# Weighing the oldest unit ahead of the newest unit's scores in a software-pipelined attention kernel

## The reference

```
def first_block(x, mem, ...):
    mem_n = layer_norm(mem, mem_ln_g, mem_ln_b)
    for i in range(DEPTH):                       # kinds A, B, C, A
        q, k, v, ..., qm = split_cols(x @ w_in, ...)      # with rope on q and k
        mix = dsa_attention | dilated_attention | moba_attention   (q, k, v)
        mk, mv = jnp.split(mem_n @ w_mem_kv[i], 2, axis=-1)
        mo = memory_attention(qm, mk, mv)
        mixed = jnp.concatenate([mix, mo], -1) @ w_out[i]
        x = layer_norm(ALPHA * x + mixed, ln1_g[i], ln1_b[i])
        x = layer_norm(ALPHA * x + swiglu(x, w_gate_up[i], w_down[i]), ln2_g[i], ln2_b[i])

def memory_attention(q, mk, mv):
    logits = jnp.einsum('bshd,bnhd->bhsn', q, mk) * (HEAD_DIM ** -0.5)
    p = jax.nn.softmax(logits, axis=-1)
    return jnp.einsum('bhsn,bnhd->bshd', p, mv)
```

## Time and profile before

| what | value |
|---|---|
| median of 3 runs | 1559.26 us (1557.5 to 1559.66) |
| span of the profiled execution, first to last instruction | 1558.9 us |
| PE busy | 1537.2 us (99%) |
| DVE busy | 1084.7 us (70%) |
| ACT busy | 757.7 us (49%) |
| chain that ended last | PE 85%, DVE 8%, ACT 3% |
| granted TensorE clock, mean | 0.998 |

### The profile page before, as it was taken

One profiled execution on the slowest core, in us unless ns is written; L12 is line 12 of the kernel. 1 busy time (PEld: TensorE's weight loads), 2 busy tenths in 40 slices (PEclk: granted clock), 3 DMA queues, 4 the chain that ended last, 5 costly groups with the idle time before them and its releaser, 6 DMA issues.

```text
span 1558.9 us, 19900 instructions
## 1 busy us (share of the span) xinstructions
PE 1537.2 (99%) x8187; PEld 1274.7 (82%) x8187; DVE 1084.7 (70%) x1422; ACT 757.7 (49%) x963; POOL 52.7 (3%) x89
## 2 busy tenths in 40 slices
PE   9999999999999999999999999999999999999997
PEld 7887788888878888888788888877888888978986
DVE  6876967656677776675966756888767677567764
ACT  5646544443444434346644343566444434474463
POOL 1100000000000000000000000000100000000010
PEclk9999999999999999999999999999999999999999
DMA  8752567645425766452476664533766546433530
GB/s 317 246 205 79 204 230 256 268 163 189 163 82 197 274 246 255 147 202 96 176 243 243 243 221 152 202 109 136 266 256 233 225 164 223 162 110 147 217 122 27
DMA packets 45898, 299.87 MB, mean 192 GB/s; under 512 B 5540, under 2 KB 5796, under 8 KB 12528
## 3 DMA queue, kind: packets, MB, share of 16 engines
q1 hardware_dynamic: 39600, 278.74, 48.9%
q0 software_dynamic: 5776, 19.01, 3.7%
q10 hardware_dynamic: 432, 0.85, 0.1%
HBM read 296.20 MB, written 2.65 MB: 192 GB/s over the span
## 4 chain that ended last, share of the span: by engine, by line
PE 85%; DVE 8%; ACT 3%; issue 2%; DMA 1%; SPq 0%; POOL 0%; POOLq 0%; DVEq 0%; ACTq 0%
PE psum L1305 53%; PE psum L1264 15%; PE psum L1299 7%; PE psum L1164 3%; DVE w_low L1779 2%; PE psum L1234 1%; PE psum L1428 1%; PE psum L1321 1%; PE psum L1382 1%; PE psum L1416 1%; PE psum L1302 1%; ACT w_high L1533 1%; DMA kv_outside<-arena 1%; DVE xt_low L1813 0%; DVE x_rows L1877 0%
## 5 line engine op out<-in xcount | busy, mean ns | idle before, releaser
L1533 ACT ACTIVATE w_high<-w_raw 128x2048 fp32r<-128x2048 f32 (+1 forms) x240 | 456.5, 1903 | 236.2 <-DMA w_raw<-in_weights 148.9
L1779 DVE TENSOR_TENSOR w_low<-w_raw,w_high 128x2048 fp32r<-128x2048 f32 (+2 forms) x240 | 530.0, 2214 | 34.1 <-ACT w_high L1533 33.3
L1305 PE MATMUL psum<-w_high,xt_high 128*128 128x512 f32 (+1 forms) x1376 | 379.3, 396 | 1.0 <-DVE x_rows L1877 0.8
L1305 PE MATMUL psum<-w_high,xt_low 128*128 128x512 f32 (+1 forms) x1376 | 368.8, 388 | 0.3 <-DVE xt_low L1813 0.3
L1305 PE MATMUL psum<-w_low,xt_high 128*128 128x512 f32 (+1 forms) x1376 | 368.1, 388 | 0.0
L1305 PEld LDWEIGHTS psum<-w_high,xt_low 128*128 128x128 f32 x1376 | 257.9, 188 | 54.9 <-DVE xt_low L1813 0.7
L1305 PEld LDWEIGHTS psum<-w_low,xt_high 128*128 128x128 f32 x1376 | 257.4, 188 | 53.9 <-DVE w_low L1765 0.4
L1305 PEld LDWEIGHTS psum<-w_high,xt_high 128*128 128x128 f32 x1376 | 250.4, 189 | 51.9 <-DVE x_rows L1877 2.4
L2109 DVE TENSOR_TENSOR arena<-arena,psum 128x256 f32<-128x256 f32 x88 | 37.0, 420 | 203.9 <-ACT arena L1665 203.5
L1665 ACT ACTIVATE arena<-psum 128x256 f32<-128x256 f32 x88 | 33.7, 383 | 217.6 <-PE psum L1305 217.6
L1264 PE MATMUL psum<-w_high,ht_high 128*128 128x512 f32 x352 | 99.9, 401 | 0.0
(11 more groups left out here) (250 smaller groups left out, 1486.2 us busy)
## 6 DMA issues: line engine op xcount, KB each, us to landing
w_raw<-in_weights SPq DMA_DIRECT2D x260, 1024.0 KB, 4.8
norm_params<-in_ln_g POOLq DMA_DIRECT2D x8, 512.0 KB, 4.1
norm_params<-in_ln_b POOLq DMA_DIRECT2D x8, 512.0 KB, 5.7
w_raw<-in_weights SPq DMA_DIRECT2D x4, 656.0 KB, 6.0
kv_outside<-arena POOLq DMA_DIRECT2D x3, 512.0 KB, 5.6
mem_kv<-kv_outside POOLq DMA_DIRECT2D x3, 512.0 KB, 3.6
norm_params<-mods_outside POOLq DMA_DIRECT2D x3, 512.0 KB, 6.7
x_rows<-in_x SPq DMA_DIRECT2D x4, 256.0 KB, 5.3
```

Source lines behind the costliest of these rows:

```text
L1305: m = e.matmul(psum[:, bank, 0:w], rows[:, kk, rb * P:rb * P + P], right[:, at:at + w], start=first, stop=last)
L1533: e.activation(K.w_hi[:, g % RING, 0:w], K.w_raw[:, r, 0:w], ACT.Copy).then_inc(K.high.hit(t), 1)
L1779: m = e.tensor_tensor(K.w_lo[:, s, 0:n], K.w_raw[:, r, 0:n], K.w_hi[:, s, 0:n].bitcast(F32), ALU.subtract)
```

## The change

One line in `pipelined` gets another order. A unit's generator stops after each of its stages, and each entry of the tuple lets one of the three units go one stage on.

```
-            for unit in (middle, new, oldest, new, middle, new):
+            for unit in (middle, oldest, new, new, middle, new):
                 if unit:
                     next(unit, None)
```

## The result

The change made the kernel slower: 1568.7 us (median of 4 runs, 1565.69 to 1571.72) against 1559.39 us before, ratio 1.0065 with a 95% interval of 1.0052 to 1.0078. The forecast was 1560.4 us with a range that ended at 1563.4. Five later runs of the same order gave 1570.46 us, ratio 1.0077 (1.0065 to 1.0090).

The account below looks back on a forecast made before the run. PE held 85% of the chain, with ACT and DVE holding parts of the attention layers. Two A layers +0.74, C +0.87, B -0.43 and the last two layers nothing made +1.2 us: 1560.4 us, range 1555.8 to 1563.4.

Parts of the forecast that it names:

- needs the transposed probabilities that DVE copies: Kind C, fifth round: the weighing right behind the product waits for L2080's copies; row maxima come +0.87 us later.
- 0.09 in the third: Kind A layers, third round: PE gains 0.09 us because transposes following masks need no switch of tile shape.
- gains of 0.27 + 0.09 and 0.11: Kind A layers, PE's chain: first round gains 0.27 + 0.09 us, second 0.11.
- the 0.93 of the fourth round: Fourth A round: row maxima 1.02 - 0.09 = 0.93 us later; less earlier gains of 0.56, the layer ends +0.37.
- In B -0.43: Kind B: 1.66 us wait goes, but the last unit's later softmax delays its transposes; the product starts 0.43 us earlier.
- 0.87 + 2.19: The 0.87: kind C's fifth-round row maxima, and the queued DVE and ACT work to the layer's end, come 0.87 us later.
- L1234's wait for L2098: Kind B: this 1.66 us wait goes almost wholly; a wait of over 1 us appears at the next transposes.
- new wait for L2080 in the fifth round: Kind C: PE newly waits some 0.6 us for DVE's copy of the transposed probabilities.
- waits of L1382 for L1650: Kind C: PE's transpose waits for ACT stay near 0.9 us in the fifth round and 0.4 in the next.
- The switch is dear: Rival, chance 0.17: weighing to scores costs 0.2 us more in each round, 2.8 in all, giving 1563.2 us.
- PE's gains hold: Rival, chance 0.13: ACT and DVE have slack, so each PE wait goes, 4.5 us in all, giving 1554.8 us.
- B keeps its whole gain: Rival, chance 0.10: in kind B DVE makes up the 0.51 us delay, giving -1.66 instead of -0.43: 1559.2 us.

Follow-up runs that it names:

- other values: Own and dilated units weigh the memory's values: 1559.51 us in the changed order, 1557.90 in the old; ratios to the kernel before 1.0004 and 0.9997.
- value rounds alone: Against the kernel before, new order only in six rounds whose values come from the product right ahead of them: 1562.79 us, ratio 1.0023.
- rounds behind: Against the kernel before, new order in the six rounds weighing values just made and the rounds following them, not those ahead: 1564.30 us, ratio 1.0037.

## Why the prediction was wrong

**The step that failed** is the list of what a weighing waits for when it stands right behind the product. For kind C the prediction wrote that it "needs the transposed probabilities that DVE copies"; for A it wrote "0.09 in the third", a gain, in the very round in which PE then waited 2.15 and 1.49 us. The values were left out. A weighing has two operands, and in six rounds the second is made by the product ahead. The trace of before shows no such wait, because scores and masks covered it (1.07 + 0.54 us in the earlier trace rows); the wait stood only in the code, and what it might cost could be told only from the row of L1922, which ended 0.10 us ahead of the weighing.

**What this makes of the sum.** In the first layer the forecast's gains of 0.27 + 0.09 and 0.11, the wait of 2.15 and the 0.93 of the fourth round give -0.47 + 2.15 + 0.93 = +2.61 (measured +2.64). In the fourth layer -0.47 + 1.49 + 0.93 = +1.95 (+1.91). In B -0.43 and the waits of 2.11 give +1.68 (+1.49). That the sums of A come out so near is in part luck: the second round gained 0.25, not 0.11 (its product starts at 140.10 in place of 140.71, and 0.36 of that is the first round's). C does not add up: 0.87 + 2.19 = +3.06, and +2.16 was measured. That PE's lateness there takes up part of what ACT and DVE lose is a guess; no run shows it.

**The forecast's own terms held in the main.** With the values' wait out of the way they came to +0.52 us in the trace (layers +0.16, -0.68, +1.04, 0.00) and to 1.6 in the medians, where +1.2 was forecast. The later maxima of the fourth A round cost 0.87 of 0.93. In B L1234's wait for L2098 went, and 1.51 us before the next transposes took its place. In C the new wait for L2080 in the fifth round was 0.61 with other values, as forecast (0.6), and 0.30 in the change. But one reading of C failed. The forecast had the waits of L1382 for L1650 stay near 0.9 in the fifth round and 0.4 in the one behind it. In the change they are, PE:

```profile
756.48 0.66 PE L1382 MATMUL psum<-ident,work 128*128 128x128 f32 x4 [0.26 <-ACT arena L1650]
...
762.39 0.66 PE L1382 MATMUL psum<-ident,work 128*128 128x128 f32 x4 [0.89 <-ACT arena L1650]
```

The wait of 0.92 did go, down to 0.26, and the one of 0.38 grew to 0.89; with other values they are 0.26 and 0.89 too, so this does not come from the values. In the fifth round of A, too, L1382 now waits 0.68 and 0.70 for L1650, where it did not before; that is about the 0.65 us that the forecast had PE lose there.

**The rivals.** "The switch is dear" fell: from weighing to scores takes 152.67 - 151.65 = 1.02 us, no more than from weighing to transposes. "PE's gains hold" fell with the waits, and also in the fourth A round by itself. "B keeps its whole gain" fell: the wait moved, as the forecast said.

**What stays open.** Kind C, as said. The clock: an equal wait of 1.87 us in B lowered it in one execution of the change and not in another, and how often it does so these few traces don't tell. The prediction's remark that the span of before lies 0.36 us under its median compared two executions; in every profiled run after it the span is some 1.8 us under that run's own time. The sum did not hang on it.

## What to carry to other kernels

Before a step is moved up against the step ahead of it, list every operand that it waits for in the code, not only the waits that the trace shows: a wait that other work covers leaves no row. Then look where the releaser stands in its engine's list, for a short evacuation is as late as whatever is queued ahead of it. And where the moved step delays that queue itself, the delays feed each other: here the rounds cost 1.8 and 4.1 us apart at equal clock, and 8.2 together. When such small differences are compared, look at the clock of each trace first, for here one place took 1.7 us from some executions and not from others.

## What the runs showed of the hardware

A pause of PE of 1.86 or 1.87 us in B was followed in three of four traces, and one of 2.14 or 2.15 us in the first layer in one of three, by some 3 to 7 us at the lower of the two clock levels (1.2 in place of 2.4 GHz; an estimate, twice the loss), costing 1.7 to 3.4 us. A single pause of 1.2 us at the place in B (value rounds alone, rounds behind) was not, nor was the one of 1.66 us in B of the kernel before; two of 1.07 and 0.73 us with one group of transposes between them, which all thirteen traces have, were in six. The prediction had priced waits by their length only.

Weighing to scores, the exchange of tile shapes that the trace before did not show, took 1.02 us for 16 matmuls (152.67 - 151.65), as weighing to transposes did. Masks to transposes, without a change of shape, took 147.93 - 147.48 = 0.45 us, the 0.45 that the prediction had estimated from three masks.
